# A woven stretch re-timed: one table of steps, a running sum in PSUM, another order inside each unit

## The chip, the cores and the metric

The kernel runs on one core of one Trainium2 chip. Its time is the device time of one execution in microseconds; the median of 3 runs of the kernel before is 2210.21 us (2208.04 to 2214.32).

## What is computed

Three transformer-like layers over 512 tokens of width 1024, all in fp32. The first two (differential and forgetting attention, SwiGLU) are not touched. The change lies in the third:

```python
proj = rms_norm(x) @ w_in             # 9 blocks: q,k,v (stick-breaking), q,f,i,g (HGRN2), two gates
# stick-breaking attention, 8 heads of 64, strictly causal
z = q.k / 8;  sp = softplus(z);  rest = reverse_cumsum(sp) - sp
w = exp(log_sigmoid(z) - rest);  o_sb = w @ v
# HGRN2, 4 heads of 128
f = lb + (1-lb)*sigmoid(f_in);  key = 1-f;  q = silu(q_in);  val = i_in
S_t = diag(f_t) S_{t-1} + key_t val_t^T;  o_t = S_t^T q_t
o_hg = rms_norm(o_t) * silu(g_in)
mixed = sigmoid(gate_sb)*(o_sb @ w_b1) + sigmoid(gate_hg)*(o_hg @ w_b2);  h = x + mixed @ w_out
```

## The kernel before, in words

A matrix product with weights is three fp32r products (hi x hi, lo x hi, hi x lo; lines 1426 to 1428): ScalarE rounds each weight slot of 128 x 1024 to `w_hi` (`hi_slot`, line 829), GpSimd subtracts to get `w_lo` (`lo_slot`, line 520). Four slots form a ring; SP fetches a slot's raw weights when TensorE has used it (`w_used`).

The input projection `in2` has 11 column blocks of 512. Blocks 2 to 10 are the woven stretch: 9 blocks x 4 slots = 36 slots, each with 8 places, and at each place TensorE makes three products of 512 columns for one token tile. Behind places it issues steps of side work, which need TensorE little and the other engines much. `SIDE` says which side units belong to a slot: `turn` (turning q and k, slots 2 and 3), `sb` (stick-breaking, slots 4 to 19), `gates` (slot 20), `hg` (HGRN2, slots 21 to 35). Inside a slot the steps of its units were spread over the 8 places by their number. Each engine walks through the same list: TensorE and VectorE as generators of steps, ScalarE and GpSimd unit by unit, with `hi_slot` and `lo_slot` of slot m+3 behind the units of slot m. VectorE also copies each finished block out of PSUM banks 0 to 3 (`in2_out`, line 1241) in every fourth slot; the first products of the next block wait for these copies tile by tile.

Stick-breaking: a unit is a head and a key block j (3 down to 0), 128 x (4-j) query columns. TensorE makes z (line 1764) at step 0 of unit u, the sums of softplus of unit u-2 (lines 1778, 1779) at step 1, the product with v of unit u-4 (line 1793) at step 2. ScalarE makes |z|, exp, ln (850 to 852); VectorE makes from them the softplus, its mask, its hi and lo parts and the exponent's first term (1269 to 1273), then subtracts the sums (1258); ScalarE takes exp; GpSimd masks. At j=0 VectorE copies the head's output out of bank 7 (line 1278).

Gates (one unit, slot 20): ScalarE's sigmoids, VectorE's forget gate (1285 to 1287), ScalarE's Ln (865), TensorE's transposes (1804).

HGRN2: a unit is a token tile and a head, 16 units. TensorE makes the sums E of log f over all levels (1841, 1842), ScalarE their exponent (890), TensorE the sum `after` (1864, 1865), GpSimd multiplies by the key (577), VectorE by q (1341). One unit later TensorE makes the level products in two halves (1857), which VectorE masks (1326) and sums (1331). Two units later it makes the output from that sum and the state (1820, 1822) and the state's product (1827). ScalarE squares and copies the output (876, 877); once a token tile `hg_norm` scales it on VectorE.

After the stretch TensorE turns the mixed rows (1432), ScalarE and VectorE split them into `xt_hi` (628) and `xt_lo` (993), and the stage `branch2` begins.

```python
for m, side in enumerate(SIDE):
    steps, made = side_steps(side), 0
    total = sum(STEPS_OF[kind] for kind, u in side)
    for n, _ in enumerate(in2_products(WOVEN[m // 4], m % 4)):
        while 8 * made < total * (n + 1):
            next(steps, None)
            made += 1
```

## Time and profile before

| what | value |
|---|---|
| median of 3 runs | 2210.21 us |
| the profiled execution, its span | 2210.44 us, 2208.5 us |
| TensorE matmul, share of the span | 97% |
| VectorE, ScalarE, GpSimd | 36%, 34%, 38% |
| granted TensorE clock, mean | 0.994 |

The time is that of a whole execution, the span runs from its first to its last profiled instruction. Shares are means over stages. PE is TensorE's matmuls, PEld its weight loads, DVE VectorE, ACT ScalarE, POOL GpSimd, SP the queue that issues the loads.

### The profile page before, as it was taken

What the parts mean: (1) busy time and instruction counts of PE and PEld (TensorE: products, weight loads), DVE (VectorE), ACT (ScalarE), POOL (GpSimd) and SP (SyncE); (2) the same over time, 40 slices, a digit from 0 to 9 for tenths busy, and PEclk for the clock granted to TensorE, in tenths of its full rate; (3) what the DMA queues carried; (4) which work ended last, traced back from release to release, by engine and by line L of the source; (5) the groups of instructions that cost most, each with busy time, mean ns of one, the idle gap of its engine ahead of it and who ended that gap; (6) DMA issues with size and microseconds to landing.
All of it is one profiled execution on the core that took longest, in us unless ns stands there. A gap on an engine that the chain in (4) does not pass through costs nothing.

```text
span 2208.5 us, 27916 instructions
## 1 busy us (share of the span) xinstructions
PE 2133.9 (97%) x10556; PEld 1764.0 (80%) x10556; DVE 785.1 (36%) x1496; ACT 750.8 (34%) x1279; POOL 845.3 (38%) x390
## 2 busy tenths in 40 slices
PE   7999999999999999999999999999788899999999
PEld 6886798888887877798888878877677789888887
DVE  5317542121014128451212014677576443121200
ACT  4226452222224136452222234544432334222211
POOL 3430134444434430244444433433344244444442
PEclk9999999999999999999999999999999999999999
DMA  6320023333333320033333322211111232333232
GB/s 194 105 86 1 1 87 115 101 97 95 95 86 105 96 76 1 28 97 96 95 95 93 103 81 68 76 49 48 48 48 39 77 106 86 96 99 100 86 100 72
DMA packets 138738, 178.25 MB, mean 81 GB/s; under 512 B 19856, under 2 KB 87696, under 8 KB 138640
## 3 DMA queue, kind: packets, MB, share of 16 engines
q1 hardware_dynamic: 137024, 175.25, 26.8%
q10 hardware_dynamic: 1616, 1.64, 0.2%
q8 instruction: 67, 1.10, 0.2%
q14 instruction: 31, 0.25, 0.0%
HBM read 174.76 MB, written 2.10 MB: 80 GB/s over the span
## 4 chain that ended last, share of the span: by engine, by line
PE 41%; issue 32%; POOL 17%; DVE 6%; ACT 2%; POOLq 0%; DMA 0%; ACTq 0%; DVEq 0%
POOL w_lo L534 17%; PE PS L1426 9%; PE PS L1428 9%; PE PS L1427 9%; PE PS L1689 3%; PE PS L1701 2%; DVE R L1331 1%; PE PS L1857 1%; PE PS L1677 1%; PE PS L1628 1%; PE PS L1764 1%; PE PS L1793 1%; DVE R L1326 1%; PE PS L1480 0%; DVE nmax L1135 0%
## 5 line engine op out<-in xcount | busy, mean ns | idle before, releaser
L534 POOL TENSOR_TENSOR w_lo<-R,w_hi 128x1024 fp32r<-128x1024 f32 (+1 forms) x288 | 678.5, 2360 | 960.3 <-ACT w_hi L615 910.5
L615 ACT ACTIVATE w_hi<-R 128x1024 fp32r<-128x1024 f32 (+1 forms) x288 | 299.9, 1044 | 961.3 <-PE PS L1428 951.5
L1426 PE MATMUL PS<-xt_hi,w_hi 128*128 128x512 f32 (+1 forms) x1216 | 460.3, 379 | 0.0
L1428 PE MATMUL PS<-xt_hi,w_lo 128*128 128x512 f32 (+1 forms) x1216 | 453.4, 373 | 0.0
L1427 PE MATMUL PS<-xt_lo,w_hi 128*128 128x512 f32 (+1 forms) x1216 | 453.3, 373 | 0.0
L1426 PE MATMUL PS<-w_hi,xt_hi 128*128 128x512 f32 x928 | 379.5, 409 | 10.8 <-DVE xt_lo L993 8.7
L1428 PE MATMUL PS<-w_hi,xt_lo 128*128 128x512 f32 x928 | 364.1, 392 | 0.0
L1427 PE MATMUL PS<-w_lo,xt_hi 128*128 128x512 f32 x928 | 363.8, 392 | 0.0
L1427 PEld LDWEIGHTS PS<-xt_lo,w_hi 128*128 128x128 f32 x1216 | 229.5, 189 | 40.1 <-issue 1.0
L1428 PEld LDWEIGHTS PS<-xt_hi,w_lo 128*128 128x128 f32 x1216 | 229.2, 189 | 40.3
L1426 PEld LDWEIGHTS PS<-xt_hi,w_hi 128*128 128x128 f32 x1216 | 229.3, 189 | 39.6 <-issue 1.0
L1197 DVE TENSOR_TENSOR h_tmp<-silu_g,PS 128x512 f32<-128x512 f32 x66 | 45.4, 688 | 539.0 <-ACT silu_g L802 537.9
L1426 PEld LDWEIGHTS PS<-w_hi,xt_hi 128*128 128x128 f32 x928 | 175.9, 190 | 45.9 <-issue 11.7
L1426 PE MATMUL PS<-w_hi,ht_hi 128*128 128x512 f32 x528 | 205.9, 390 | 0.8 <-POOL w_lo L534 0.8
L1428 PEld LDWEIGHTS PS<-w_hi,xt_lo 128*128 128x128 f32 x928 | 175.5, 189 | 37.9
L1427 PE MATMUL PS<-w_lo,ht_hi 128*128 128x512 f32 x528 | 205.4, 389 | 0.0
L1428 PE MATMUL PS<-w_hi,ht_lo 128*128 128x512 f32 x528 | 205.4, 389 | 0.0
L1427 PEld LDWEIGHTS PS<-w_lo,xt_hi 128*128 128x128 f32 x928 | 176.0, 190 | 31.7 <-issue 0.7
L520 POOL TENSOR_TENSOR w_lo<-raw,w_hi 128x1024 fp32r<-128x1024 f32 x40 | 97.8, 2445 | 132.5 <-ACT w_hi L829 119.7
L1426 PEld LDWEIGHTS PS<-w_hi,ht_hi 128*128 128x128 f32 x528 | 99.1, 188 | 22.7 <-POOL w_lo L534 2.1
L1428 PEld LDWEIGHTS PS<-w_hi,ht_lo 128*128 128x128 f32 x528 | 99.1, 188 | 20.5
L1427 PEld LDWEIGHTS PS<-w_lo,ht_hi 128*128 128x128 f32 x528 | 99.1, 188 | 20.4
(237 smaller groups left out, 2167.8 us busy)
## 6 DMA issues: line engine op xcount, KB each, us to landing
R<-in_w_in SPq DMA_DIRECT2D x56, 512.0 KB, 3.7
R<-in_w_gate SPq DMA_DIRECT2D x88, 256.0 KB, 2.8
R<-in_w_up SPq DMA_DIRECT2D x88, 256.0 KB, 3.0
R<-in_w_down SPq DMA_DIRECT2D x40, 512.0 KB, 3.7
raw<-in_w_in SPq DMA_DIRECT2D x36, 512.0 KB, 3.7
R<-in_w_out SPq DMA_DIRECT2D x24, 512.0 KB, 3.7
R<-in_w_ffn_gate SPq DMA_DIRECT2D x44, 256.0 KB, 2.8
R<-in_w_ffn_up SPq DMA_DIRECT2D x44, 256.0 KB, 3.0
```

Of the source, the lines that this page charges most:

```text
L520: nc.gpsimd.tensor_tensor(w_lo[:, r], raw[:, r], w_hi[:, r].bitcast(F32), ALU.subtract).then_inc(lo_ready, 1)
L534: nc.gpsimd.tensor_tensor(w_lo[:, r, 0:subs, :], raw_of(stage, lap)[:, r, 0:subs, :], w_hi[:, r, 0:subs, :].bitcast(F32), ALU.subtract).th ...
L615: nc.scalar.activation(w_hi[:, r, 0:subs, :], raw_of(stage, lap)[:, r, 0:subs, :], ACT.Copy).then_inc(hi_ready, 1)
L1197: V.tensor_tensor(h_tmp[:, :], silu_g[:, j, :], PS[:, 4 * s + 2 + j, :], ALU.mult).then_inc(h_mul, 1)
L1326: V.tensor_tensor(hg_a[:, ls, :], psum_a, PAIRS[:, ls, :], ALU.mult).then_inc(a_read, 1)
L1331: V.tensor_reduce(hg_at[:, v % 2, :], hg_a.rearrange("p l t -> p t l"), AX.X, ALU.add).then_inc(a_sum, 1)
L1426: mm(out_, a_hi, b_hi, start=start, stop=False)
L1427: mm(out_, a_hi, b_lo, start=False, stop=False)
L1428: return mm(out_, a_lo, b_hi, start=False, stop=stop)
L1628: last = nc.tensor.transpose(PS[0:rows, bank, t * P:(t + 1) * P], src[:, t, :], ident[:, :])
L1689: mm(PS[:, u % 4, 0:upto], q, kk, start=True, stop=False)
L1701: last = mm(PS[:, 6 + n % 2, 0:width], probT[:, n % 2, j * P:(j + 1) * P], vals, start=j == 0, stop=j == i)
```

## The change

One table, `STEPS_AT`, says how many side steps come behind each place, and `spread` fills it evenly over a run of slots: `sb` over slots 4 to 18, `hg` over 21 to 35. The gates become two units: `forget` (ScalarE's sigmoids, VectorE's forget gate and two multiplies, slots 18 to 20) and `gates` (the transposes and their split, slot 20); the blocks for g and the values change places. In `sb` the sums come at step 0, and the product with v and z together at step 1; bank 6 keeps the sums of the head's later blocks, to which the table UPTO adds a block's whole columns and AFTER the own block's. In `hg` the sums E stand first, the output product stands with the first half of the levels, the state's product with the second; VectorE multiplies the output by its gate straight out of PSUM in place of ScalarE's copy, and ScalarE does the norm's scaling. The first four `xt_hi` of `branch2` stand ahead of the last weight slot.

```diff
--- before.py
+++ after.py
 WOVEN = range(2, 11)
 SB_UNITS, HG_UNITS = 32, 16
 SB_AFTER, HG_AFTER = 4, 3
-SIDE = [[] for _ in range(4 * len(WOVEN))]
-for _n in range(8):
-    SIDE[2 + _n // 4].append(("turn", _n))
-for _n in range(SB_UNITS + SB_AFTER):
-    SIDE[4 + 4 * _n // 9].append(("sb", _n))
+STEPS_OF = {"turn": 1, "sb": 3, "forget": 4, "gates": 4, "hg": 6}
+SLOTS = 4 * len(WOVEN)
+SIDE = [[] for _ in range(SLOTS)]
+STEPS_AT = [[0] * 8 for _ in range(SLOTS)]
+
+
+def spread(units, first, last):
+
+    total = sum(STEPS_OF[kind] for kind, u in units)
+    made, places = 0, 8 * (last - first)
+    for place in range(places):
+        upto = total * (place + 1) // places
+        STEPS_AT[first + place // 8][place % 8] += upto - made
+        made = upto
+    step = 0
+    for unit in units:
+        place = next(p for p in range(places) if total * (p + 1) // places > step)
+        SIDE[first + place // 8].append(unit)
+        step += STEPS_OF[unit[0]]
+
+
+spread([("turn", n) for n in range(8)], 2, 4)
+spread([("sb", n) for n in range(SB_UNITS + SB_AFTER)], 4, 19)
+SIDE[18].append(("forget", 0))
 SIDE[20].append(("gates", 0))
-for _n in range(HG_UNITS + HG_AFTER):
-    SIDE[21 + 15 * _n // (HG_UNITS + HG_AFTER)].append(("hg", _n))
-STEPS_OF = {"turn": 1, "sb": 3, "gates": 4, "hg": 7}
+for _m, _n in ((19, 4), (19, 6), (20, 1), (20, 3), (20, 5), (20, 6), (20, 7), (20, 7)):
+    STEPS_AT[_m][_n] += 1
+spread([("hg", n) for n in range(HG_UNITS + HG_AFTER)], 21, SLOTS)
+WOVEN_SIDE = [unit for _side in SIDE for unit in _side]
...
-                            load_lap(stage, LAP0[stage] + lap, lap, 0)
+                            load_lap(stage, LAP0[stage] + lap, IN2_COLUMNS[lap] if stage == "in2" else lap, 0)
...
-            def gates_side():
+            def forget_side():
                 act.preload_act_table(ACT.Sigmoid)
-                act.wait_ge(in2_ev, 4 * (4 - WOVEN[0]) + 4)
+                act.wait_ge(in2_ev, 4 * (5 - WOVEN[0]) + 4)
                 act.wait_ge(av_ev, 8)
                 act.wait_ge(av_mm, len(units2))
+                nc.scalar.activation(KHT, KHT, ACT.Sigmoid).then_inc(sig_done, 1)
                 nc.scalar.activation(q_sig, QHT, ACT.Sigmoid).then_inc(sig_done, 1)
-                nc.scalar.activation(KHT, KHT, ACT.Sigmoid).then_inc(sig_done, 1)
-                act.wait_ge(in2_ev, 4 * (6 - WOVEN[0]) + 4)
                 nc.scalar.activation(g_sig, GG, ACT.Sigmoid).then_inc(sig_done, 1)
                 act.preload_act_table_set(EXP_TABLE)
                 act.wait_ge(f_sum, 1)
                 nc.scalar.activation(logf_t, logf_t, ACT.Ln).then_inc(log_done, 1)
+
+            def gates_side():
...
             def hg_side(u):
                 w = u - 2
                 if 0 <= w < len(hg_units):
-                    i, h = hg_units[w]
                     act.wait_ge(oh_mm, w + 1)
-                    nc.scalar.activation(SQ3, PS[:, 7, 0:P], ACT.Square, accum_out=small[:, 0, w:w + 1])
-                    nc.scalar.activation(MIX[:, i, CW + h * P:CW + (h + 1) * P], PS[:, 7, 0:P], ACT.Copy).then_inc(oh_ev, 1)
-                    if h == 3:
-                        act.wait_ge(oh_ev, w + 1)
-                        cols = slice(4 * i, 4 * i + 4)
-                        link(nc.scalar.activation(small[:, 3, cols], small[:, 0, cols], ACT.Ln, scale=1.0 / P, bias=EPS))
-                        nc.scalar.activation(small[:, 1, cols], small[:, 3, cols], ACT.Exp, scale=-0.5).then_inc(y0_ready, 1)
-                        roots[0] += 1
+                    nc.scalar.activation(SQ3, PS[:, 7, 0:P], ACT.Square, accum_out=small[:, 0, w:w + 1]).then_inc(oh_sq, 1)
                 if u < len(hg_units):
                     act.wait_ge(e_mm, u + 1)
                     if u == 0:
                         act.wait_ge(lf_dve, 4)
-                    if u >= 2:
-                        act.wait_ge(oh_mm, u - 1)
                     nc.scalar.activation(hg_e[u % 2][:, 0:LEVELS + 1, :], psum_e, ACT.Exp).then_inc(e_exp, 1)
-                    if hg_units[u][0] < T - 1:
-                        act.wait_ge(after_mm, u + 1)
-                        nc.scalar.activation(hg_e[u % 2][:, LEVELS + 1, :], PS[:, 4, 0:P], ACT.Exp).then_inc(after_exp, 1)
+                if 0 <= w < len(hg_units) and hg_units[w][1] == 3:
+                    act.wait_ge(oh_sq, w + 1)
+                    cols = slice(w - 3, w + 1)
+                    link(nc.scalar.activation(small[:, 3, cols], small[:, 0, cols], ACT.Ln, scale=1.0 / P, bias=EPS))
+                    nc.scalar.activation(small[:, 1, cols], small[:, 3, cols], ACT.Exp, scale=-0.5).then_inc(y0_ready, 1)
+                    roots[0] += 1
+                if u < n_states:
+                    act.wait_ge(after_mm, u + 1)
+                    nc.scalar.activation(hg_e[u % 2][:, LEVELS + 1, :], PS[:, 4, 0:P], ACT.Exp).then_inc(after_exp, 1)
                 v = u - 1
                 if 0 <= v < n_states:
                     act.wait_ge(ket_mm, v + 1)
                     nc.scalar.activation(hg_ket[:, v % 2, :], PS[:, 7, 256:256 + P], ACT.Copy).then_inc(ket_ev, 1)
+                w = u - 3
+                if w >= 0 and hg_units[w][1] == 3 and hg_units[w][0] < T - 1:
+                    hg_norm(hg_units[w][0])
+
+            def hg_norm(i):
+                act.wait_ge(hg_rstd, i + 1)
+                for h in range(4):
+                    part = MIX[:, i, CW + h * P:CW + (h + 1) * P]
+                    ins = nc.scalar.activation(part, part, ACT.Copy, scale=small[:, 5, 4 * i + h:4 * i + h + 1])
+                ins.then_inc(xn_ready, 1)
...
                 hi_slot(*in2_slot(m + 3))
+            transposed_hi("branch2", ks=range(4))
             hi_slot(*in2_slot(len(SIDE) + 3))
-            transposed_hi("branch2")
+            hg_norm(T - 1)
+            transposed_hi("branch2", ks=range(4, KD))
...
-            in2_to = {2: VS, 3: QHT, 4: KHT, 5: VAL, 6: GG, 7: GATE_SB[:, :, 0:CW], 8: GATE_SB[:, :, CW:D],
+            in2_to = {2: VS, 3: QHT, 4: KHT, 5: GG, 6: VAL, 7: GATE_SB[:, :, 0:CW], 8: GATE_SB[:, :, CW:D],
...
             def sb_side(u):
-                yield
                 v = u - 2
                 if 0 <= v < len(units2):
                     h, j = units2[v]
                     n = SEQ - P * j
                     lt = sb_l[v % 6][:, 0:n]
                     dve.wait_ge(rest_mm, v + 1)
-                    V.tensor_tensor(lt, lt, PS[:, 6, 0:n], ALU.subtract).then_inc(arg_done, 1)
-                yield
+                    V.tensor_tensor(lt, lt, PS[:, 6, j * P:SEQ], ALU.subtract).then_inc(arg_done, 1)
+                yield
+                v = u - 4
+                if v >= 0 and units2[v][1] == 0:
+                    h = units2[v][0]
+                    dve.wait_ge(av_mm, v + 1)
+                    V.tensor_copy(MIX[:, :, h * HD:(h + 1) * HD],
+                                  PS[:, 7, 0:T * HD].rearrange("p (t d) -> p t d", d=HD)).then_inc(av_ev, 1)
                 if u < len(units2):
                     h, j = units2[u]
                     n = SEQ - P * j
...
+            def forget_side():
+                dve.wait_ge(sig_done, 1)
                 for h in range(4):
                     link(V.tensor_scalar(logf_t[:, h, :], KHT[:, h, :], lbc[:, 5, h:h + 1], lbc[:, 4, h:h + 1], ALU.mult, ALU.add))
-                link(V.tensor_scalar(KHT, logf_t, -1.0, 1.0, ALU.mult, ALU.add))
+                V.tensor_scalar(KHT, logf_t, -1.0, 1.0, ALU.mult, ALU.add).then_inc(key_done, 1)
+                dve.wait_ge(key_done, 1)
                 V.tensor_scalar(logf_t, logf_t, 2.0 ** -62, None, ALU.max).then_inc(f_sum, 1)
+                yield
+                dve.wait_ge(sig_done, 2)
                 link(V.tensor_tensor(QHT, QHT, q_sig, ALU.mult))
+                yield
                 dve.wait_ge(sig_done, 3)
-                V.tensor_tensor(GG, GG, g_sig, ALU.mult)
+                link(V.tensor_tensor(GG, GG, g_sig, ALU.mult))
+                yield
+                yield
+
...
             def hg_norm(i):
                 cols = slice(4 * i, 4 * i + 4)
-                dve.wait_ge(oh_ev, 4 * i + 4)
+                dve.wait_ge(oh_sq, 4 * i + 4)
                 link(V.tensor_scalar(small[:, 2, cols], small[:, 0, cols], 1.0 / P, EPS, ALU.mult, ALU.add))
-                link(refine(cols))
-                for h in range(4):
-                    part = MIX[:, i, CW + h * P:CW + (h + 1) * P]
-                    ins = V.scalar_tensor_tensor(part, part, small[:, 5, 4 * i + h:4 * i + h + 1],
-                                                 GG[:, i, h * P:(h + 1) * P], ALU.mult, ALU.mult)
...
             def hg_side(u):
                 yield
+                yield
                 v, w = u - 1, u - 2
+                if 0 <= w < len(hg_units):
+                    i, h = hg_units[w]
+                    cols = slice(h * P, (h + 1) * P)
+                    dve.wait_ge(oh_sq, w + 1)
+                    V.tensor_tensor(MIX[:, i, CW + h * P:CW + (h + 1) * P], PS[:, 7, 0:P], GG[:, i, cols],
+                                    ALU.mult).then_inc(oh_ev, 1)
+                if 0 <= v < len(hg_units):
+                    dve.wait_ge(a_mm, 2 * v + 1)
+                    V.tensor_tensor(hg_a[:, 0:4, :], psum_a, PAIRS[:, 0:4, :], ALU.mult).then_inc(a_read, 1)
+                yield
+                yield
...
+                    if j < T - 1:
+                        later = slice(sp_at[j + 1], sp_at[j + 1] + n - P)
+                        for sp in (sp_hi, sp_lo):
+                            mm(PS[:, 6, (j + 1) * P:SEQ], sums_r[:, UPTO, :], sp[:, h % 2, later], start=False, stop=False,
+                               skip_group_check=True)
+                    pe.wait_ge(sp_done, v + 1)
+                    own = slice(sp_at[j], sp_at[j] + n)
+                    mm(PS[:, 6, j * P:SEQ], sums_r[:, AFTER, :], sp_hi[:, h % 2, own], start=j == T - 1, stop=False,
+                       skip_group_check=True)
+                    mm(PS[:, 6, j * P:SEQ], sums_r[:, AFTER, :], sp_lo[:, h % 2, own], start=False, stop=True,
+                       skip_group_check=True).then_inc(rest_mm, 1)
                 yield
                 v = u - 4
...
+                if u < len(units2):
+                    h, j = units2[u]
+                    n = SEQ - P * j
+                    if u >= 2:
+                        pe.wait_ge(sp_done, u - 1)
+                    mm(PS[:, 4 + u % 2, 0:n], KST[:, h // 2, j * P:(j + 1) * P], QST[h % 2][:, h // 2, j * P:SEQ],
+                       start=True, stop=True).then_inc(z_mm, 1)
+                yield
                 yield
...
+                yield
+                if 0 <= w < len(hg_units):
+                    iw, hw = hg_units[w]
+                    val = VAL[:, iw, hw * P:(hw + 1) * P]
+                    if w == 0:
+                        pe.wait_ge(in2_ev, 4 * (6 - WOVEN[0]) + 4)
+                    pe.wait_ge(a_sum, w + 1)
+                    pe.wait_ge(ket_ev, states_before(w + 1))
+                    if w >= 1:
+                        pe.wait_ge(oh_ev, w)
+                        pe.wait_ge(state_done, states_before(w))
+                    last = mm(PS[:, 7, 0:P], hg_at[:, w % 2, :], val, start=True, stop=iw == 0)
+                    if iw > 0:
+                        last = mm(PS[:, 7, 0:P], hg_e[w % 2][:, UPTO, :], hg_state[:, hw, :], start=False, stop=True)
+                    last.then_inc(oh_mm, 1)
+                if 0 <= v < len(hg_units):
+                    hg_levels(v, 0)
+                yield
+                if u < n_states:
+                    pe.wait_ge(e_exp, u + 1)
+                    table = sums_r[:, AFTER, :]
+                    mm(PS[:, 4, 0:P], lf[0], table, start=True, stop=False)
+                    mm(PS[:, 4, 0:P], lf[1], table, start=False, stop=True).then_inc(after_mm, 1)
+                yield
+                if 0 <= w < n_states:
+                    pe.wait_ge(oh_ev, w + 1)
+                    mm(PS[:, 7, P:2 * P], hg_ket[:, w % 2, :], VAL[:, iw, hw * P:(hw + 1) * P], start=True,
+                       stop=True).then_inc(kv_mm, 1)
+                if 0 <= v < len(hg_units):
+                    hg_levels(v, 1)
...
```

## Rows read from the trace of the kernel before

**Rows 1.** The page's part 1: busy us, share of the span, instructions.
```profile
PE 2133.9 (97%) x10556; PEld 1764.0 (80%) x10556; DVE 785.1 (36%) x1496; ACT 750.8 (34%) x1279; POOL 845.3 (38%) x390
```
**Rows 2.** Busy time by stretch: us, engines, granted clock, DMA share, GB/s.
```profile
1399.00:1551.50 152.50, 147.68 (x766) 122.36 (x764) 117.00 (x216) 74.61 (x145) 56.59 (x49) 0.99 0.20 56
1551.50:1562.90 11.40, 1.74 (x10) 1.13 (x9) 7.78 (x9) 8.78 (x6) 1.23 (x1) 0.68 0.16 46
1562.90:1572.00 9.10, 9.10 (x42) 7.62 (x43) 5.15 (x6) 3.34 (x5) 0.00 (x0) 0.84 0.01 2
1572.00:1739.40 167.40, 148.21 (x793) 119.40 (x792) 105.31 (x127) 47.96 (x111) 72.97 (x32) 0.99 0.16 48
1739.40:1750.20 10.80, 5.81 (x26) 4.83 (x25) 5.12 (x13) 3.37 (x5) 4.28 (x2) 0.68 0.72 243
```
**Rows 3.** TensorE's waits, 1380 to 1760: waiter, releaser, us, times, longest.
```profile
PE PS L1820 <- DVE R L1331: 14.8, 16, 1.4
PE PS L1804 <- ACT R L865: 9.7, 1, 9.7
PE PS L1426 <- DVE xt_lo L993: 5.0, 1, 5.0
PE PS L1793 <- DVE R L1278: 4.8, 4, 1.7
PE PS L1827 <- ACT R L877: 2.5, 4, 0.6
```
**Rows 4.** Timeline, sums of one unit: start us, us, engine, line.
```profile
1542.18 0.39 PE L1778 MATMUL PS<-R2R,sums_r 128*128 128x512 f32 x1
...
1542.63 0.33 PE L1778 MATMUL PS<-R2R,sums_r 128*128 128x384 f32 x1
```
**Rows 5.** Timeline, softplus chain of the widest unit, alone and beside GpSimd.
```profile
1442.64 0.63 ACT L852 ACTIVATE R<-R 128x512 f32<-128x512 f32 x1
...
1499.47 0.69 DVE L1269 SCALAR_TENSOR_TENSOR G<-PS,R 128x512 f32<-128x512 f32 x1
...
1501.60 0.68 DVE L1273 SCALAR_TENSOR_TENSOR R<-PS,R 128x512 f32<-128x512 f32 x1
...
1534.17 0.69 DVE L1269 SCALAR_TENSOR_TENSOR G<-PS,R 128x512 f32<-128x512 f32 x1 [0.43 <-ACT R L852]
...
1535.17 2.40 POOL L520 TENSOR_TENSOR w_lo<-raw,w_hi 128x1024 fp32r<-128x1024 f32 x1 [4.73 <-ACT w_hi L829]
1535.23 2.63 DVE L1271 TENSOR_SCALAR R2R<-G 128x512 fp32r<-128x512 f32 x1
...
1538.64 0.68 DVE L1273 SCALAR_TENSOR_TENSOR R<-PS,R 128x512 f32<-128x512 f32 x1
```
**Rows 6.** Timeline of the gates.
```profile
1556.06 2.29 DVE L1285 TENSOR_SCALAR R<-R,lbc 128x512 f32<-128x512 f32 x4 [2.81 <-ACT R L860]
...
1560.92 1.91 ACT L865 ACTIVATE R<-R 128x2048 f32<-128x2048 f32 x1 [1.79 <-DVE R L1287]
```
**Rows 7.** Timeline of one HGRN2 unit.
```profile
1594.63 2.37 POOL L520 TENSOR_TENSOR w_lo<-raw,w_hi 128x1024 fp32r<-128x1024 f32 x1 [0.96 <-ACT w_hi L829]
...
1595.33 2.75 DVE L1341 TENSOR_TENSOR R<-R 128x1024 f32<-128x1024 f32 x1
...
1598.54 1.03 ACT L890 ACTIVATE R<-PS 128x1024 f32<-128x1024 f32 x1 [2.18 <-PE PS L1842]
...
1601.52 1.05 PE L1857 MATMUL PS<-R 128*128 128x128 f32 x8
...
1603.33 2.00 DVE L1331 TENSOR_REDUCE R<-R 128x128 f32<-128x1024 f32 x1
```
**Rows 8.** Timeline of the step to branch2.
```profile
1743.76 1.06 ACT L829 ACTIVATE w_hi<-raw 128x1024 fp32r<-128x1024 f32 x1 [4.89 <-DMA raw<-in_w_branch]
1744.72 2.41 ACT L628 ACTIVATE xt_hi<-PS,gcol 128x512 fp32r<-128x512 f32 x4
...
1746.32 0.77 PE L1426 MATMUL PS<-w_hi,xt_hi 128*128 128x512 f32 x1 [4.99 <-DVE xt_lo L993]
```

153 lines of the change are left out of this document (47 added, 106 removed).

## The prediction, made blind

> **What bounds the kernel now.** I read the busy line of the page first: TensorE is busy 97% of the span [rows 1]. Only what TensorE itself executes, and what it waits for, can move the time. The table by stage comes next, cut at the edges of the woven stretch [rows 2]. There the reader sees four losses: VectorE at 117.0 of 152.5 us in the stick-breaking part; 11.4 us with 1.74 us of products where the gates are made; 148.2 busy of 167.4 us in the HGRN2 part; 5.8 of 10.8 us at the step to the next stage. The last view, TensorE's own waits, gives these holes their releasers [rows 3]: 14.8 us in 16 waits for the level sum, 9.7 us in one wait for the forget gate's Ln, 5.0 us for the first `xt_lo` after the stretch, 4.8 us in four waits for the copy that frees bank 7, and 2.5 us before the state product.
>
> Idle time also costs afterwards. Behind the 9.7 us hole the granted clock is 0.84 over 9.1 us, and it is 0.68 over the 10.8 us that contain the 5.0 us hole [rows 2]; the granted clock has two levels, 2.4 GHz and half of it, so (1-0.84) x 9.1 = 1.5 us of work time is lost in the first. In the second, products run only from 1746.3 on [rows 8]; 0.32 x 10.8 = 3.5 us of clock, of which about half falls into the hole: 1.8 us. The two long parts show 0.99, which is 1.5 us and 1.7 us. A product of 512 columns takes 0.45/2 = 0.225 us from start to start [rows 4]; with 24 in a slot and the small gaps I take 5.46 us a slot, 0.68 us for each of its eight places, wherever the side work leaves TensorE alone.
>
> **The change part by part.** The sum is made against the profiled execution, 2210.4 us with a span of 2208.5; the median of the runs shown is 2210.2.
>
> *Running sums.* Before, unit j of a head sums the blocks j..3 with two products each: 2 x (1280+768+384+128) = 5120 columns a head. Afterwards it adds one block's columns with the table UPTO onto what bank 6 already holds: 2 x (896+640+384+128) = 4096. That is 1024 x 8 = 8192 columns less. At 0.45 us for 1024 columns [rows 4] it is **3.6 us** of TensorE time, on the path everywhere. Bounds: 3.0 to 4.5.
>
> *fp32 products side by side.* The number of products is unchanged. A group of eight 128-column records of the level products starts at 1601.52 and its last ends after 1.05 us [rows 7]; 8 x 0.11 and the drain of one fill that, so no price for the neighbour's type is left to save. I take 0; bounds -1 and +5 (0.1 us for each of the some 50 borders that go, one record's length in [rows 7]).
>
> *Stick-breaking part: other order, 15 slots for 16.* Number of products unchanged. The wait for bank 7 goes: VectorE's copy stands ahead of its softplus chain, TensorE needs it three steps later. Gone: 4.8 us [rows 3] and 1.5 us of clock [rows 2] = 6.3. What is late next is the chain of the widest unit (j=0, 512 columns). Before, z was issued seven steps ahead of the sums that need its softplus; now five steps. Five steps at 120/108 places are 5.6 places = 3.8 us. With the side products between (about 3 us) the sums of j=0 come some 5 us after z ends. VectorE needs: ScalarE's three passes at 0.63 = 1.9 us, then the chain, 1499.47 to 1502.28 = 2.8 us (both [rows 5]), and next the subtraction of the unit before it, 0.7, for which TensorE also waits: 5.4 us. So 0.45 us late, eight times: 3.6. When GpSimd's split holds the chain it takes 1534.17 to 1539.32, 5.15 us, 2.35 more [rows 5]; in before this meets the widest unit in 3 of 8 heads. Part of the delay goes into slack, so 5 us for the stretch. New stalls **8.6 us** (bounds 2 and 19 = 8 x 2.35), net -2.3.
>
> *Gates over two slots.* Products now run while the chain works, from place 6 of slot 18 to place 5 of slot 20: 15 x 0.68 = 10.3 us. The chain itself, from the end of the last attention product: copy and wait 1.0; VectorE's forget step comes behind two `in2_out` copies, that is at 4.2, and takes 1556.06 to 1560.92 = 4.9 us [rows 6], to 9.1; Ln 1.9 to 11.0. That would leave under 1 us. But two other `in2_out` copies of slot 19 stand in VectorE's queue behind this work, and TensorE's first products of tiles 2 and 3 in slot 20 wait for them. It reaches tile 2 at 7.6 and gets it at 9.1 + 0.7 = 9.9: 2.3 us. The multiply of QHT by its sigmoid (as many elements as the four operations of 2.29 us in [rows 6], and put at the same) stands ahead of the last copy: 12.9, where TensorE is at 10.6: 2.3 us more. Sum 4.6, plus 0.5 for the split of the last gate ahead of the first E, plus 2.5 for the clock. Together **7.6** for 9.7 + 1.5 = 11.2: 3.6 gained (bounds 0 and 9). On the clock, the row says that a 9.7 us hole is followed by half speed, and that 16 holes of about 0.9 us cost little (0.99). Two holes of 2.3 us lie between; I take 2.5 us between 0 and 5.
> The Trainium skill ("TensorE: Matmul & The Clock Gate", HAM oscillation) has recurring waits put the engine back to the slow clock each time. By it each hole would be paid again at half speed, and the item would stand at its upper bound; no run so far shows holes of this length in pairs.
>
> *HGRN2 part.* The level sum's consumer moves four steps behind the level products (was two) and E's products stand between: from the start of the second half of the levels to the sum's end it is 1601.52 to 1605.33 = 3.8 us [rows 7], the new distance is 0.9 + 4 x 0.72 + 0.9 + 0.5 = 5.2 us. The waits of 14.8 and 2.5 us go, and 1.7 of clock: 19.0. What is late next: (a) ScalarE squares unit w before the exponent of unit u, and w's product now comes two steps after E, so the 1.03 us exponent [rows 7] ends 0.2 us after TensorE wants its `after` product, 12 times: 2.4. (b) VectorE's loop. From the start of half 0 of the levels: half 1 at 2.9, its masked read and the sum 1.8 + 2.0 later, to 6.7 (1601.52, 1603.33 and 2.00 in [rows 7]), then the 1.22 us multiply by QHT, to 8.0. The pace of TensorE is 6.3 places x 0.68 + 4.1 of side products = 8.4, so this is hidden. But ScalarE makes the next slot's w_hi behind the unit's last copy, so GpSimd's split runs from 5.75 to 8.1, and the multiply, like the one in [rows 7] (split 1594.63 to 1597.00, multiply ends 1598.08), ends 1.1 us after the split: 9.2. Against 8.4 + 0.2 that is 0.65 us, in about 12 of 16 units: 7.8. The four copies of tiles in each fourth slot fit VectorE's idle time. The output's multiply by the gate straight out of PSUM (some 0.3 us for 128 columns, from 0.69 for 512 in [rows 5]) replaces work of the same size on VectorE and a copy on ScalarE; ScalarE is 48 of 167 us busy [rows 2], nothing. New stalls **10.2** (bounds 3 and 24), gain 8.8.
>
> *Step to branch2.* Before, ScalarE stands before the four `xt_hi` at the DMA of the last weight slot (1743.76 + 1.06) and begins them at 1744.72; the first product comes at 1746.32 [rows 8], 1.6 us after. Now they stand ahead of that wait and begin about 1.7 us after the transposes' first, at 1741.1 on this clock: product at 1742.7, 1.4 us idle instead of 5.0. The last token tile's norm must be in time: VectorE's four small steps, then ScalarE's four scalings at 0.3, are done some 7.4 us after slot 35 ends; TensorE asks for them after two k blocks, at 8.8. Behind it the shorter idle spell should leave the clock up or cost 0.4. **5.0** gained of 6.8 (bounds 2.5 and 6.8).
>
> SP's queue, GpSimd's queue: w_hi and w_lo of slot m+3 keep their order behind the side units of slot m and have three slots of lead; the DMAs are tied to `w_used` as before. Nothing.
>
> New waits are thus 8.6 + 7.6 + 10.2 + 1.8 = 28.2 us for 6.3 + 11.2 + 19.0 + 6.8 = 43.3 of before. Sum: 3.6 - 2.3 + 3.6 + 8.8 + 5.0 = 18.7; 2210.4 - 18.7 = **2191.7**, and 2192 rounded for the median.
>
> **Rivals.**
> *A, the new stalls stay out.* If the splits meet the wide chain rarely and the gates' holes leave the clock alone, new waits are 2 + 5 + 3 + 1.5 = 11.5 and the gain is 3.6 + 43.3 - 11.5 = 35: 2175. For it: VectorE has 152.5 - 117.0 = 35 us idle in the stick-breaking part [rows 2]. Against: the order inside a unit, not the amount of work, sets the two loops.
> *B, a wash.* The waits change their names: TensorE gives back in the softplus and gate chains what it saves. Stick-breaking 12, gates 9, HGRN2 18, end 3: 42 us of new waits against the 46.9 that go, gain 5: 2205. For it: all four new loops are tighter than the old ones. Against: the two largest old waits were faults of order and nothing of their kind is added.
> *C, slower: GpSimd's split on VectorE's two loops.* Each split that starts during the widest unit's chain adds 2.35 us, and in the HGRN2 part 1.5 us to the multiply by QHT where the whole delay reaches TensorE. If the new rhythm puts one in every head (19 + 3.6) and in each unit (24 + 2.4), with the gates 9 and clock falls 4, new waits are 22.6 + 26.4 + 13 = 62 us against 46.9: 2210 + 15 = 2225. It decides from 47 us of new waits on. For it: behind a split of 2.40 us one rounding of 512 columns took 2.63 us, nearly as long as the whole chain of 2.8 without one [rows 5]. Against: before, such meetings were 3 of 8 in the widest unit, and slots of 9 us and units of 4 us drift against each other.
> The Trainium skill ("SBUF — State Buffer", SBUF: two separate sides) calls the pair of ports that VectorE and GpSimd share an exclusive lock, held for a whole instruction. By it a meeting costs the rest of the 2.4 us and never less, as the trace shows with 2.35; sharing in proportion would cost half, and C would then fall away.
> *D, only the end and the sums work*: 8.6 us: 2202; inside the range.
>
> **How the numbers follow.** My case 0.60, A 0.17, B with D 0.16, C 0.07. This kernel's runs lie within 0.3% of each other, so 6.6 us is what can be told from no change. Faster by more than that, under 2203.6: my case, A, and a third of B and D: 0.82. Within: 0.13. Slower: 0.05, the part of C beyond it. The range 2172 to 2205 takes in A and most of B.
>
> **What would show it.** In the profile after: the wait of the output product for the level sum gone or under 3 us; the 9.7 us wait gone, and in its place two waits of about 2.3 us of a weight product for VectorE's copy at the start of slot 20; waits of the sums for VectorE's softplus chain once a head; a wait of the level products for the multiply by QHT; the first branch2 product about 3.3 us after slot 35 instead of 6.9; the sums' columns down by a fifth. I am wrong if the waits in the HGRN2 part stay near 19 us, if the gates' hole stays whole because the Ln is not ready, or if the clock is at half in more than some 10 us of the stretch.

## The result, and the profile after

The changed kernel takes 2194.73 us (median of four runs, 2192.98 to 2196.20) against 2209.36 us (four runs, 2208.04 to 2214.32): a ratio of 0.9931 [0.9918, 0.9944]. The forecast was 2192, so the direction, the size and the range held. The term for the stick-breaking part did not; the others came within 2 us or better than foretold. One of e2's four runs took 3586.49 us at a granted clock of 0.555, and e2's time below is taken from the other three.

Read the busy line of the page first (engine, busy us, share of the span, instructions); it answers to [rows 1].

```profile
PE 2125.9 (97%) x10508; PEld 1758.4 (80%) x10508; DVE 778.9 (35%) x1496; ACT 749.1 (34%) x1279; POOL 848.6 (39%) x390
```

48 matmul records are gone, six for each of eight heads: the running sums. Next come the stretches, cut at the same events as in [rows 2] (first z, end of the last attention product, first E, end of slot 35, and then 10.8 us); columns are us, then busy us and count of TensorE, its weight loads, VectorE, ScalarE and GpSimd, granted clock, DMA share, GB/s.

```profile
1403.00:1554.50 151.50, 137.86 (x686) 110.33 (x685) 114.38 (x211) 72.21 (x143) 52.16 (x47) 0.99 0.18 51
1554.50:1575.70 21.20, 16.98 (x73) 12.97 (x72) 16.48 (x17) 13.84 (x12) 6.77 (x2) 0.92 0.23 65
1575.70:1730.20 154.50, 142.44 (x791) 120.43 (x792) 98.46 (x131) 46.70 (x107) 73.16 (x32) 1.00 0.16 50
1730.20:1741.00 10.80, 9.15 (x52) 7.53 (x51) 6.31 (x10) 5.63 (x11) 4.45 (x2) 1.00 0.69 243
```

The first two must be read as one, because products of the old slots now run where the gates are made: from the first z to the first E it is 172.7 us, and before it was 172.6. The HGRN2 part takes 154.5 us for 167.1. The first product of branch2 starts 3.2 us after slot 35, not 6.9. Its clock stays at 1.00, while before the half clock lasted from 1743.4 for 6.8 us. From that product to the end of the span it is 460.9 us for 462.2: 1.3 us more comes back behind the edge. That makes -0.1 + 12.6 + 3.7 + 1.3 = 17.5 us. The two profiled spans differ by only 14.2 (2208.5 and 2194.3), because this execution began with a half-clock spell of 6.8 us at 41.5, far ahead of the changed code: its first z stands at 1403.0, against 1399.7 before and 1399.5 in e7 below, which runs the same code up to there. Those 3.3 us are not the change's: two of the four runs of the changed kernel have spans of 2191.2 and 2191.5.

The stretches themselves differ from one execution to the next, by the clock alone. From the first z to the first E the changed kernel, e3, e4 and e7 run the same code: 172.7, 172.7, 174.4 and 171.7 us, with 6.8, 6.8, 10.2 and 5.1 us of products at half clock in them. The HGRN2 part took 154.5 us here and 154.4 in e4, without a half-clock spell, and 156.0 in e1 and e7, each with one of 3.4 us; e7 differs there in one product's place. So 1 to 2 us in one stretch of one profile can be luck, and 1.5 us of the HGRN2 part's gain are.

The last view is what TensorE waited for from 1380 to 1760 (waiter, releaser, us, times, longest). It answers to [rows 3].

```profile
PE PS L1807 <- DVE R L1291: 11.0, 10, 2.4
PE PS L1465 <- DVE R L1275: 7.2, 6, 2.0
PE PS L1859 <- DVE R L1382: 6.9, 9, 1.0
PE PS L1900 <- ACT R L904: 3.5, 2, 2.2
PE PS L1465 <- DVE xt_lo L1027: 1.3, 1, 1.3
PE PS L1859 <- DVE R L1357: 0.6, 1, 0.6
```

All five of the old names are gone or small. In their place stand the running sums behind VectorE's subtraction (L1807), a weight product behind VectorE's tile copies (L1465, four of its six waits ahead of the first E), the level products behind the multiply by QHT (L1859), and `after` behind ScalarE (L1900).

**The largest new wait.** The timeline of a widest unit, from z to the running sums (start us, duration, engine, line; in brackets the idle time ahead and its releaser), is to be laid beside [rows 5].

```profile
1446.53 1.08 PE L1834 MATMUL PS<-R 128*128 128x512 f32 x2
...
1449.61 0.69 DVE L1308 SCALAR_TENSOR_TENSOR G<-PS,R 128x512 f32<-128x512 f32 x1 [2.07 <-ACT R L875]
...
1450.60 2.39 POOL L543 TENSOR_TENSOR w_lo<-raw,w_hi 128x1024 fp32r<-128x1024 f32 x1 [5.33 <-ACT w_hi L852]
1450.66 2.61 DVE L1310 TENSOR_SCALAR R2R<-G 128x512 fp32r<-128x512 f32 x1
...
1454.65 0.54 DVE L1291 TENSOR_TENSOR R<-R,PS 128x384 f32<-128x384 f32 x1
...
1455.24 0.62 PE L1807 MATMUL PS<-R2R,sums_r 128*128 128x384 f32 x2 [2.44 <-DVE R L1291]
```

z ends at 1447.6 and TensorE wants its sums at 1452.8, 5.2 us later, as worked out. GpSimd's split starts during the chain and L1310 takes 2.61 us. The subtraction of the unit before, which frees bank 6, stands behind the whole chain in VectorE's queue, and ends at 1455.2. In the six heads where no split meets it this rounding takes 0.43 us. So without the split the sums would be 2.2 us earlier, and TensorE nearly in time (an estimate from these rows).

**The gates** (timeline, answers to [rows 6]):

```profile
1563.35 0.68 DVE L1275 COPY R<-PS 128x512 f32<-128x512 f32 x1
...
1563.95 2.28 DVE L1325 TENSOR_TENSOR R<-R 128x2048 f32<-128x2048 f32 x1
1564.09 0.50 PE L1465 MATMUL PS<-w_hi,xt_hi 128*128 128x512 f32 x1 [2.03 <-DVE R L1275]
...
1566.27 0.69 DVE L1275 COPY R<-PS 128x512 f32<-128x512 f32 x1
...
1567.02 0.57 PE L1465 MATMUL PS<-w_hi,xt_hi 128*128 128x512 f32 x1 [1.96 <-DVE R L1275]
```

The Ln (L887) has no TensorE wait behind it any more, as the list of waits above shows. What TensorE waits for twice is a copy of a finished tile out of PSUM, one behind the forget gate's multiplies, the other behind the multiply by QHT's sigmoid (L1325): the two holes foretold, 2.0 us each for 2.3.

**The step to branch2** (answers to [rows 8]):

```profile
1731.78 2.42 ACT L651 ACTIVATE xt_hi<-PS,gcol 128x512 fp32r<-128x512 f32 x4 [1.97 <-PE PS L1471]
...
1733.40 0.47 PE L1465 MATMUL PS<-w_hi,xt_hi 128*128 128x512 f32 x1 [1.33 <-DVE xt_lo L1027]
...
1734.52 1.06 ACT L852 ACTIVATE w_hi<-raw 128x1024 fp32r<-128x1024 f32 x1 [0.32 <-DMA raw<-in_w_branch]
```

ScalarE makes the four xt_hi ahead of the weight slot's DMA instead of behind it; 1.33 us idle for 4.99.

### The profile page after: what moved, and what is told of

The parts are those of the page before. It is cut to its first block, busy times and chain, and to the rows that moved or that the text cites. A ratio compares the mean times of both kernels' runs of the same rounds, so it can differ in the third digit from the quotient of the medians.

```text
span 2194.3 us, 27783 instructions
## 1 busy us (share of the span) xinstructions
PE 2125.9 (97%) x10508; PEld 1758.4 (80%) x10508; DVE 778.9 (35%) x1496; ACT 749.1 (34%) x1279; POOL 848.6 (39%) x390
## 4 chain that ended last, share of the span: by engine, by line
PE 38%; issue 33%; POOL 17%; DVE 9%; ACT 3%; POOLq 0%; ACTq 0%; DVEq 0%
POOL w_lo L557 17%; PE PS L1465 9%; PE PS L1467 8%; PE PS L1466 8%; PE PS L1728 3%; PE PS L1740 2%; PE PS L1859 1%; DVE R L1374 1%; PE PS L1716 1%; DVE R2R L1311 1%; PE PS L1667 1%; DVE R L1382 1%; PE PS L1834 1%; PE PS L1826 0%; DVE R L1370 0%
## 5 line engine op out<-in xcount | busy, mean ns | idle before, releaser
L1465 PE MATMUL PS<-xt_hi,w_hi 128*128 128x512 f32 (+1 forms) x1216 | 458.4, 377 | 0.0
L1465 PE MATMUL PS<-w_hi,xt_hi 128*128 128x512 f32 x928 | 375.6, 405 | 16.7 <-DVE R L1275 7.2
L1465 PEld LDWEIGHTS PS<-xt_hi,w_hi 128*128 128x128 f32 x1216 | 229.1, 188 | 40.4 <-issue 1.0
L1465 PEld LDWEIGHTS PS<-w_hi,xt_hi 128*128 128x128 f32 x928 | 175.6, 189 | 55.3 <-DVE R L1275 9.8
L1465 PE MATMUL PS<-w_hi,ht_hi 128*128 128x512 f32 x528 | 205.9, 390 | 0.8 <-POOL w_lo L557 0.8
L1465 PEld LDWEIGHTS PS<-w_hi,ht_hi 128*128 128x128 f32 x528 | 99.1, 188 | 22.4 <-POOL w_lo L557 2.1
```

Source lines behind the costliest of these rows:

```text
L1465: mm(out_, a_hi, b_hi, start=start, stop=False)
```

## The experiments

The theory: TensorE paces the stretch; the splits alone do not make the new waits, the order within a unit does, and a split only lengthens what is already late. The rival: GpSimd's splits make them (rival C's mechanism). The theory is e1's, the rival e2's. The experiments ran beside the kernel before and not beside the changed one. Its median there was 2210.26, 2209.6 and 2208.35 us in three sets of runs, so a difference to the changed kernel's 2194.73 is known to some 2 us.

**e1.** z one step earlier, at the head of its unit and so ahead of the sums of unit u-2:

```diff
 # sb_steps(u), first step
+                if u < len(units2):
+                    mm(PS[:, 4 + u % 2, 0:n], KST[...], QST[...], ...).then_inc(z_mm, 1)
                 ... # UPTO sums and own sums of unit v
-                if u < len(units2): ... # z, as above
```

> The changed kernel with one edit: TensorE issues z of unit u at step 0, ahead of the sums of unit u-2, instead of behind the product with v at step 1. Theory (the sums wait for VectorE's softplus chain because z comes late): z is about 1.9 us earlier in each unit, so TensorE's wait of the sums for that chain falls from 11.0 us (10 times) to under 4, the one half-speed spell of 3.4 us in this part goes, and the time falls by 6 to 10 us, to about 2187. Rival 1 (the chain is late because VectorE as a whole is full in this part, in throughput): the wait stays near 11 us and the time at 2194. Rival 2 (fp32 products side by side save time at their borders, and z now stands apart from the product with v): up to 3 us lost, 2197.

Measured: 2179.48 us (2178.28 to 2180.86), 0.9862 [0.9841, 0.9883] of the kernel before, 15.3 us under the changed kernel.

```profile
1400.80:1537.00 136.20, 134.45 (x689) 110.16 (x688) 111.48 (x212) 72.20 (x143) 52.56 (x47) 1.00 0.20 58
```
```profile
PE PS L1803 <- DVE R L1312: 0.5, 2, 0.3
...
PE PS L1814 <- DVE R L1291: 0.3, 1, 0.3
```

The first is the window of the stick-breaking part (in the rest of the way to the first E the clock is 0.84), the second TensorE's waits. The 11.0 us are 0.8 (L1803 is z, L1814 the sums), the tile copies' 7.2 are 5.7, the clock is 1.00 in this window, and the splits run as before. The direction was right and the size too small. The stretch from first z to first E is 14.6 us shorter. Of this 10.2 us are L1807's and 1.5 the copies'. The clock gives 1.0: the spell behind the sums is gone, but the one at the gates lasted 6.8 us for 3.4, so products ran at half clock for 4.8 us instead of 6.8. The last 1.9 us lie in no wait. TensorE has seven fewer waits there (3 for 10), and at the 0.2 us beyond each that e7 shows below these would give 1.4 (an estimate).

**e2.** No split in the 34 slots of the stretch: GpSimd's subtraction is left out and ScalarE writes zeros into w_lo (so the low part of these weights is missing from the result).

```diff
                 nc.scalar.activation(w_hi[:, r], raw[:, r], ACT.Copy).then_inc(hi_ready, 1)
+                act.wait_ge(hi_ready, 4 * lap + r + 1)
+                nc.scalar.activation(w_lo[:, r], raw[:, r], ACT.Copy, scale=0.0).then_inc(lo_act, 1)
-                        lo_slot(*in2_slot(m + 3))
+                        lo_mark(*in2_slot(m + 3))   # waits for lo_act, counts lo_ready
```

> The changed kernel, but in the woven stretch GpSimd's subtraction that makes w_lo (2.4 us on each of the last 34 slots) is left out: ScalarE writes zeros into w_lo right behind w_hi (1 us more on ScalarE a slot), GpSimd only passes the signal on. The low part of these weights is left out of the product. Theory (GpSimd's split blocks VectorE's softplus chain and its multiply by q): the softplus operations never take over 1 us, the wait of the sums falls from 11.0 to about 4 us, that of the level products for the multiply from 6.9 to under 1, the time by 10 to 15 us, to about 2182. Rival (order alone makes the loops late): waits fall by less than a third and the time stays above 2191; ScalarE's extra microsecond may even cost 2.

Measured: 2176.60 us (three runs, 2176.57 to 2181.73), 0.9862 [0.9833, 0.9892]. That is 18.1 us under the changed kernel by the medians and 15.2 by the two ratios; from the first z (1400.13 here) to the end of the span the two profiles differ by 16.6. I take some 16.

```profile
PE PS L1818 <- DVE R L1302: 4.1, 5, 1.4
...
PE PS L1870 <- DVE R L1393: 0.9, 4, 0.4
```

L1818 is the changed kernel's L1807, L1870 its L1859. The sums' wait falls from 11.0 to 4.1 us and the level products' from 6.9 to 0.9. So of the 11.0 us, 4.1 belong to the order alone, and 6.9 need both: e1 removes them with the splits in place, e2 with the order in place. Kept apart by shape (line, names, shape and count, then busy us and mean ns, then idle time before them), the groups show where. The changed kernel, then e2:

```profile
L1807 PE MATMUL PS<-R2R,sums_r 128*128 128x384 f32 x16 | 4.9, 391 | 6.7 <-DVE R L1291 6.7
L1807 PE MATMUL PS<-R2R,sums_r 128*128 128x256 f32 x16 | 3.7, 313 | 3.3 <-DVE R L1291 3.2
L1807 PE MATMUL PS<-R2R,sums_r 128*128 128x128 f32 x16 | 2.9, 261 | 1.2 <-DVE R L1291 1.2
```
```profile
L1818 PE MATMUL PS<-R2R,sums_r 128*128 128x384 f32 x16 | 5.0, 390 | 4.5 <-DVE R L1302 4.1
L1818 PE MATMUL PS<-R2R,sums_r 128*128 128x256 f32 x16 | 3.2, 280 | 0.0
L1818 PE MATMUL PS<-R2R,sums_r 128*128 128x128 f32 x16 | 2.7, 248 | 0.0
```

The 384 columns are those that the widest unit (j=0) adds, 256 and 128 those of j=1 and j=2. Without splits only the widest unit is late; with them 4.4 us fall on the two narrower ones. In the HGRN2 part the split is the cause (6.0 of 6.9). The edit is not free: with ScalarE's extra writes the wait of `after` grows from 3.5 to 4.6 us, so the splits' price is rather more than what e2 shows. Neither theory is whole; the wait needs a chain without slack and a split on it.

**e8.** The same omission in the kernel before:

> The kernel before, with GpSimd's subtraction for w_lo left out of the last 34 slots of the woven stretch and zeros written by ScalarE (the low part of these weights is left out of the product). Theory (the old order had slack against the split, its waits came from the places of the steps): the 14.8 us of waits for the level sum stay at 13 or more, the 9.7 us of the gates stay, the 4.8 us of waits for bank 7 fall to 2 or less; the time falls by 3 to 7 us, to about 2205, against 15.6 us by the same edit on the changed kernel. Rival (the split cost the kernel before as much): 10 us or more, under 2200.

Measured: 2203.96 us, 0.9977 [0.9967, 0.9986], that is -5.6 us.

```profile
PE PS L1831 <- DVE R L1342: 14.7, 16, 1.3
PE PS L1815 <- ACT R L876: 9.8, 1, 9.8
```

These two large waits of [rows 3] stay as they were, and bank 7's is off the list. The wait for the first `xt_lo` grows from 5.0 to 6.2 us, because ScalarE's last write of zeros (1.06 us at 1737.45) stands ahead of `xt_hi`. The splits cost the old order 5.6 us and the new order some 16 (the expectation's 15.6 is from the median of all four runs of e2). So the change made the kernel more sensitive to them, which is rival C's mechanism at about a third of the 43 us (19 and 24) that C put on it.

**e3.** The output product back at the head of the unit, ahead of E:

```diff
 # hg_steps(u), first step
+                if 0 <= w < len(hg_units):
+                    ... # hg_at x VAL, hg_e x hg_state into bank 7, then_inc(oh_mm)
-                # the same, two steps later
```

> The changed kernel with one edit: in an HGRN2 unit TensorE issues the output product at step 0, ahead of the sums E, where it was in the kernel before, instead of at step 2 beside the first half of the level products. Theory (the place of this product made the 14.8 us of waits for the level sum): the waits come back, more than 0.9 us each because the levels' second half now stands at step 4, two steps ahead: 16 x 1.3 = 20 us; the 3.5 us of waits for ScalarE's exponent go; the level products' wait of 6.9 us falls to about 2. Net +11, about 2206. Rival (the step spacing, not this product's place, removed the waits): under 5 us of waits for the level sum, the time within 3 us of 2194.

Measured: 2201.26 us, 0.9963 [0.9951, 0.9976], +6.5 us over the changed kernel's median.

```profile
PE PS L1874 <- DVE R L1374: 18.5, 15, 1.3
```
```profile
1572.50:1735.70 163.20, 142.58 (x790) 1.00 0.16 47
```

The wait for the level sum is back (18.5 us for 14.8 before) and takes the place of the level products' 6.9 and 2.7 of the 3.5 of `after`. The net of the waits is +8.9, and the stretch (second fence: the window of the HGRN2 part, TensorE alone) grows by 8.7, to 163.2 from 154.5. That is nearer to the 11 expected than the time is; 3.2 us of the difference to the changed kernel's profile lie in that one's start-up. Against the expectation the level sum waits 18.5 us for 20, and the level products' wait is gone instead of 2.

**e7.** The state product, which the change had put just ahead of the second half of the level products, stands beside the `after` product instead:

```diff
                     mm(PS[:, 4, 0:P], lf[1], table, start=False, stop=True).then_inc(after_mm, 1)
+                if 0 <= w < n_states:
+                    ... # hg_ket x VAL into bank 7, then_inc(kv_mm)
```

> The changed kernel with the state's fp32 product moved one step ahead, beside the two short fp32r products of 'after', so that it no longer stands next to the second half of the level products. Theory 1 (fp32 next to fp32 saves a border): the group of state product, levels and turned key takes 1.23 us now; apart, the state product costs 0.43 us by itself as in the kernel before, 0.2 more, 12 times: +2.5 us, 2197. Theory 2 (the 0.2 us was an exposed weight load behind a wait that was only just met; the neighbour's type is free): the state product costs 0.22 to 0.25 us alone too, the time stays at 2194.7 within 1 us.

Measured: 2193.39 us, 0.9932 [0.9916, 0.9949]; not told apart from the changed kernel. The rows do tell. The kernel before, then e7 (PEld is the load of the weights of the product on the same line):

```profile
1596.08 0.40 PE L1428 MATMUL PS<-w_hi,xt_lo 128*128 128x512 f32 x1
...
1596.41 0.30 PEld L1827 LDWEIGHTS PS<-R 128*128 128x128 f32 x2 [0.37 <-ACT R L877]
1596.41 0.49 PE L1827 MATMUL PS<-R 128*128 128x128 f32 x2
...
1596.97 0.40 PE L1427 MATMUL PS<-w_lo,xt_hi 128*128 128x512 f32 x1
```
```profile
1691.33 0.39 PE L1467 MATMUL PS<-w_hi,xt_lo 128*128 128x512 f32 x1
1691.34 0.42 PEld L1904 LDWEIGHTS PS<-R 128*128 128x128 f32 x2
1691.57 0.38 PE L1904 MATMUL PS<-R 128*128 128x128 f32 x2
...
1692.02 0.40 PE L1466 MATMUL PS<-w_lo,xt_hi 128*128 128x512 f32 x1
```

From the product ahead of it to the second one behind it are 0.89 us in the first and 0.69 in the second. Two products of 0.23 us lie in that time, so the state product costs 0.43 us before and 0.23 in e7 (0.22 in the changed kernel, beside fp32 products). In e7 its neighbours are of the other type as before, but nothing holds its weight load: it starts at 1691.34, under the product ahead. Before, the load waits for ScalarE's copy (L877) and starts only at 1596.41, with the product. Eight of the 12 units of the kernel before show this 0.88 or 0.89; the other four have a wait of 0.63 on the list. So the 0.2 us belongs to a wait met only just before, behind which the weights are loaded in the open, and not to the type of the product beside it. The forecast's 0 for "side by side" stands, for this operation.

**e4.** The first four xt_hi again behind the last weight slot:

```diff
-            transposed_hi("branch2", ks=range(4))
             hi_slot(*in2_slot(len(SIDE) + 3))
+            transposed_hi("branch2", ks=range(4))
```

> The changed kernel with one edit: ScalarE makes the first four xt_hi of branch2 behind the last weight slot again, as before. Theory: they wait for that slot's DMA, the first product of branch2 comes 5.0 us after the transposes instead of 1.3, and the clock falls for 3.4 to 6.8 us behind it: +3.7 for the idle time and +1.5 to 2 for the clock, about 2200. Rival (the idle time alone moves, branch2 is bound later by its own loads or by the gates' sigmoids and takes it back): under +1, 2195.

Measured: 2199.43 us, 0.9952 [0.9938, 0.9966], +4.7 us.

```profile
PE PS L1465 <- DVE xt_lo L1027: 5.0, 1, 5.0
```
```profile
1729.30:1736.20 6.90, 1.95 (x18) 0.80 0.75 253
```

The 5.0 us wait, the 6.9 us from slot 35 to the first product and the slow clock all return (the second fence is that window). This part of the change is shown by itself, with its size.

**e6 and e9.** The running sums undone in the changed kernel (e6), and done alone in the kernel before (e9):

```diff
-                        mm(PS[:, 6, (j + 1) * P:SEQ], sums_r[:, UPTO, :], sp[:, h % 2, later], start=False, ...)
-                    mm(PS[:, 6, j * P:SEQ], sums_r[:, AFTER, :], sp_hi[:, h % 2, own], ...)   # and sp_lo
+                    for jj in range(j, T):
+                        table = sums_r[:, AFTER if jj == j else ONES, :]
+                        mm(PS[:, 6, jj * P:SEQ], table, sp_hi[:, h % 2, part], ...)          # and sp_lo
```

> The changed kernel with the running sum undone: unit j sums blocks j to 3 with two products each again, 5120 instead of 4096 columns a head, all behind the wait for the softplus chain. Theory: 8192 columns x 0.445 ns = 3.6 us more, and the part that was issued ahead of the wait (0.35 us for the widest unit, eight times) no longer fills it: +3.6 to +6.5, about 2200. Rival (in this part TensorE waits for VectorE 11.0 us, so fewer columns were no gain): within 1 us of 2194.7.

> The kernel before with the running sum alone: one block's columns with the table UPTO onto what bank 6 holds, then the own block's, issued at the old place. Theory: in the old order the sums hardly wait for the softplus chain, so the 8192 columns show in full: -3.6 us (0.9984), a little more or less by the waits for bank 7. Rival (the sums' work was hidden in the waits for bank 7, 4.8 us): under 1 us.

Measured: e6 2200.58 us, 0.9961 [0.9947, 0.9975], +5.9 us on the changed kernel; e9 2204.9 us, 0.9982 [0.9972, 0.9992] of the kernel before, -3.45 us. Alone the term comes out at 3.45 us; the interval runs from 1.8 to 6.2, so it takes in the 3.6 us that the columns give and leaves out the rival's "under 1". Bank 7's wait grows there from 4.8 to 5.7 us.

In e6 the stretch from first z to first E grows by 4.8 us while its sums' wait falls by 0.8. Of the 4.8 us 0.9 are clock: products ran at half clock for 8.7 us instead of 6.8. With the fallen waits some 1 us is left beyond the columns' 3.6, and is not placed. The HGRN2 part, whose code is unchanged, takes 1.6 us more, with one half-clock spell of 3.4 us as in e1 and e7.

**e5 and e10.** The best version. e5 is e1, and: the second gate step moved from (19, 6) to (20, 0), so that the second tile copy stands ahead of it; in ScalarE's queue the weight slot ahead of the copy of the turned key; the norm of a token tile one unit later. e10 is e5 with the multiply of GG by its sigmoid behind the last gate's split.

```diff
-((19, 4), (19, 6), (20, 1), (20, 3),
+((19, 4), (20, 0), (20, 1), (20, 3),
 # hg_side
+                if last_of is not None:
+                    hi_slot(*in2_slot(last_of + 3))
                 if 0 <= v < n_states:
                     act.wait_ge(ket_mm, v + 1)
-                w = u - 3
+                w = u - 4
                 if w >= 0 and hg_units[w][1] == 3 and hg_units[w][0] < T - 1:
 # e10 only: V.tensor_tensor(GG, GG, g_sig, ALU.mult) moved behind lf's split of h == 3
```

> The changed kernel with z ahead of the sums (2179.5 us alone) and three more edits of order. (a) The second gates step (VectorE's multiply of q) moves from place 6 of slot 19 to place 0 of slot 20, behind the last tile copy: the second of the two 2.0 us waits at the start of slot 20 goes, -2.0. (b) ScalarE makes the next slot's w_hi ahead of the copy of the turned key, not behind it, so GpSimd's split ends before VectorE's multiply by q begins: the level products' wait of 6.9 us falls to under 1.5, -5.5. (c) ScalarE scales a token tile's output one unit later, so that it doesn't wait for VectorE's multiply ahead of the next exponent: the 3.5 us of waits before the sum 'after' go, and half a spell of slow clock, -4. Theory: the parts add up to -11.5, 2168. Rival (each wait removed shows the next one, since VectorE's loop has no slack behind it): half of it, 2174.

> The fastest kernel so far (2166.8) with VectorE's multiply of GG by its sigmoid moved behind the split of the last gate. It took 4.37 us there beside GpSimd's split, and the first sums E of HGRN2 waited 2.27 us for the parts of the gate behind it. Theory: that wait goes to under 0.3 us, nothing new comes: -2.1 us, 2164.7. Rival (the multiply then holds VectorE where the tile copies or the first unit need it): the wait reappears as one of the level products, under 0.7 us gained.

Measured: e5 2166.79 us (2166.23 to 2168.85), 0.9809 [0.9792, 0.9825]; e10 2166.03 us (2165.57 to 2166.92), 0.9807 [0.9792, 0.9821]. e5 lies at the 2168 expected and not at the rival's 2174. TensorE's waits of e5, then of e10:

```profile
PE PS L1468 <- DVE R L1278: 3.8, 5, 2.0
PE PS L1862 <- DVE R L1385: 3.3, 8, 0.7
PE PS L1878 <- DVE R2R L1338: 2.3, 1, 2.3
```
```profile
PE PS L1863 <- DVE R L1386: 3.8, 9, 0.7
...
PE PS L1879 <- DVE R2R L1336: 0.3, 1, 0.3
```

`after`'s 3.5 us are gone, one of the two gate holes too, the level products wait half as long, and no half-clock spell falls into the stretch. The first E of e5 waited 2.3 us behind VectorE, where the GG multiply held the queue for 4.4:

```profile
1549.88 4.37 DVE L1331 TENSOR_TENSOR R<-R 128x2048 f32<-128x2048 f32 x1
```

e10 takes that wait away, but its time is only 0.8 us under e5's, less than these runs tell apart; the 2.1 expected is neither shown nor excluded. Half a microsecond of it stands at the level products instead (3.8 for 3.3). The three edits beside e1's are told apart only by their waits; none was run alone. The first 2.0 us tile copy of slot 20 stays in both and was not worked on.

## Why the prediction was right, and where its sum was not

- *Running sums, 3.6.* Right: 3.45 alone (e9), 5.9 with the rest (e6), where 2.5 us of the profile's growth are clock (0.9 and 1.6).
- *fp32 side by side, 0.* The one place tried (e7) shows no price of the type; the other borders were not measured.
- *Stick-breaking, new stalls 8.6: the term that failed.* Measured 15.2: 11.0 for the sums, 1.7 and 0.8 for tile copies, 1.7 for one half-clock spell of 3.4 us (none in e7, two in e4, with the same code). The order's own share was put at 8 x 0.45 = 3.6 and is 4.1 (e2). The splits' share was put at 5, because they met the widest unit in three of eight heads before; it is 6.9. In the changed kernel they lengthen that unit's chain in two heads (1450.66 and 1504.42). The number of meetings hardly changed: of the chain's 96 masks, roundings and low parts 14 take over 1 us in the kernel before and 13 in the changed one, six of these at j=1 for four before. What was wrong is that only j=0 was worked out. At j=0 the splits add 2.6 us (6.7 - 4.1), less than the 5; at j=1 and j=2 they add 4.4, for which there was no term, because without a split those units are in time (e2). The tile copies and the clock had no term at all; the copies join the same queue behind the same chain. This item was to cost 2.3 net and cost 8.7 (15.2 for the 4.8 and 1.7 of before).
- *Gates, new 7.6.* Measured 6.0: 2.0 and 2.0 for the two copies, 0.3 for the first E, and 1.7 of clock where 2.5 was taken. The upper bound of 5 for the clock came from a rule of the Trainium skill ("TensorE: Matmul & The Clock Gate", HAM oscillation), by which each hole is paid again at half speed. The trace shows one spell of 3.4 us for the pair of holes, at 1567.3, and so do e2, e3 and e4. In e1, e6 and e7 the same pair had one of 6.8 us, some 2.5 us of clock, which is the value taken. Two spells, one for each hole, stand in no profile.
- *HGRN2, new 10.2, gain 8.8.* New waits 11.8 (6.9 + 0.6 + 3.5 + 0.8), gain 12.6. The multiply by QHT was put at 7.8, and is 6.9; 0.6 is the level products' wait for VectorE's masked read (L1357), which had no term. The 2.4 for `after` is 3.5, but from another cause: not 12 times 0.2 us behind an exponent, but two waits of 2.2 and 1.3. There ScalarE's scaling (L926) stands ahead of the exponent and has itself stood 4.36 us behind VectorE's small steps (first row below). The old waits were 1.7 us more than the term counted (1.3 for the multiply by QHT at L1857, 0.4 for `after`): 19.0 + 1.7 - 11.8 = 8.9. Of the other 3.7, 1.6 to 2.4 are the state products at 0.2 us each, which had no term (an estimate from e7's rows, for eight or all 12), and the rest I can't place. That the clock gave back all of its 1.7 was luck: in e1, e6 and e7 a spell of 3.4 us stands in this part, as in the kernel before, and the gain would be 11.
- *Step to branch2, 5.0.* Measured 3.7 + 1.3 = 5.0; e4 gives 4.7.

Together 17.5 for 18.7, before the 3.3 us of start-up in the profiled run; the medians differ by 14.6. Misses of opposite sign (stick-breaking 6.6 worse, the gates 1.6 and HGRN2 3.8 better than foretold) nearly cancel, so the time is better than the working deserves.

The first row is ScalarE's scaling with its wait. The others, from another unit, show a split that leaves the level sum ahead of it untouched and lengthens the multiply by QHT from 1.22 to 2.04 us:

```profile
1635.96 1.28 ACT L926 ACTIVATE R<-R,small 128x128 f32<-128x128 f32 x4 [4.36 <-DVE small L987]
```
```profile
1587.91 2.02 DVE L1374 TENSOR_REDUCE R<-R 128x128 f32<-128x1024 f32 x1
...
1588.59 2.40 POOL L543 TENSOR_TENSOR w_lo<-raw,w_hi 128x1024 fp32r<-128x1024 f32 x1 [0.25 <-ACT w_hi L852]
...
1590.03 2.04 DVE L1382 TENSOR_TENSOR R<-R 128x1024 f32<-128x1024 f32 x1
```

The rivals: A (2175) did not happen. e5 comes to waits of its size (11.9 us on its list, A's 11.5) by another order, and to 2166.79 us. B had stick-breaking at 12 (15.2), gates at 9 (6.0) and HGRN2 at 18 (11.8): too low for the first, too dark for the others. C's mechanism is real (e2, some 16 us) and stayed far from its 62 us of waits: the new waits of the four parts are 15.2 + 6.0 + 11.8 + 1.3 = 34.3. D (8.6 us in all) is excluded by the HGRN2 part's gain of 11 to 12.6.

## What to carry to other kernels

When steps of one engine are respread, work out for each consumer the distance in time from its producer and compare it with the full chain behind it, including what else stands in the helper engine's queue; moving z by one step was worth 15 us, as much as the whole change. Do this for every size of unit, once alone and once with the longest operation that can block the helper (here 2.4 us of GpSimd): the units that are in time alone but have less slack than that carry the cost that is easily missed. Before two profiles are subtracted, lay them on a common event ahead of the change: here 3 of 14 us were the start-up's. Then count the half-clock spells in each: four profiles of the same code from first z to first E lay 2.7 us apart by them alone.
